# Page numbers read without a range check per page, the page table clamped once beforehand

## The reference

```
mla_past = cache_mla[li, page_table].reshape(db, PAST_LEN, MLA_KV_LORA + MLA_ROPE)
old = cache_kv[li, page_table, :, 0:2].reshape(B, PAST_LEN, 2, G, d)   # keys and values to compress
page = page_table[bi, ip // sub][..., None]                            # of the selected blocks
kp = cache_kv[li, page, rows, 2, gsel]
vp = cache_kv[li, page, rows, 3, gsel]
```

## Time and profile before

| | us |
|---|---|
| median of 3 runs | 3161.9 |
| lowest and highest run | 3148.9, 3181.5 |
| span of the profiled execution | 3163.9 |

### The profile page before, as it was taken

One profiled execution on the slowest core, in us unless ns is written; L12 is line 12 of the kernel. 1 busy time (PEld: TensorE's weight loads), 2 busy tenths in 40 slices (PEclk: granted clock), 3 DMA queues, 4 the chain that ended last, 5 costly groups with the idle time before them and its releaser, 6 DMA issues. The chain is left out here.

```text
span 3163.9 us, 69355 instructions
## 1 busy us (share of the span) xinstructions
PE 2792.1 (88%) x25382; PEld 1845.6 (58%) x25382; DVE 1249.9 (40%) x3286; ACT 875.3 (28%) x2098; POOL 124.2 (4%) x217
## 2 busy tenths in 40 slices
PE   6999888899982699799997999799999998888878
PEld 4556455666651544455466879667676765555534
DVE  3111455455546521111000000275757576666633
ACT  1111444333332010101000000164646464444400
POOL 0000000011102000000000000000000000221100
PEclk9999999999995699899987999798989898899989
DMA  4001100377753131511054766400000001777732
GB/s 174 22 12 49 29 1 1 117 222 220 227 159 48 38 133 62 211 45 41 31 157 138 231 221 190 116 2 2 2 1 2 2 2 50 224 229 219 228 123 77
DMA packets 312746, 320.72 MB, mean 101 GB/s; under 512 B 72420, under 2 KB 289940, under 8 KB 312089
## 3 DMA queue, kind: packets, MB, share of 16 engines
q1 hardware_dynamic: 226120, 233.29, 24.2%
q10 hardware_dynamic: 86290, 83.01, 8.6%
HBM read 289.15 MB, written 30.27 MB: 101 GB/s over the span
## 5 line engine op out<-in xcount | busy, mean ns | idle before, releaser
L2207 PE MATMUL bank<-cm_room 64*64 64x114 f32 (+1 forms) x4608 | 297.0, 441 | 6.6 <-DMA cm_room<-cache_nsa_kv 6.6
L2207 PEld LDWEIGHTS bank<-cm_room 64*64 64x64 f32 x4608 | 254.6, 163 | 45.9 <-DMA cm_room<-cache_nsa_kv 7.5
L2554 ACT ACTIVATE np_p<-bank,np_nmax 128x640 f32<-128x640 f32 (+7 forms) x256 | 179.3, 700 | 230.1 <-DVE np_nmax L2609 229.0
L2027 PE MATMUL bank<-cm_room 128*128 128x512 f32 (+3 forms) x576 | 224.9, 551 | 0.0
L2493 PEld LDWEIGHTS bank<-kv,np_pT 128*64 128x64 f32 x4224 | 149.3, 142 | 90.1 <-ACT np_pT L2563 42.0
L2493 PE MATMUL bank<-kv,np_pT 128*64 128x64 f32 x4224 | 185.1, 233 | 2.3 <-ACT np_pT L2563 2.2
L2609 DVE TENSOR_REDUCE np_nmax<-bank 128x1 f32<-128x640 f32 (+7 forms) x256 | 181.2, 708 | 8.8
L2479 PE MATMUL bank<-ident,np_p 128*128 128x128 f32 x1056 | 179.2, 296 | 3.7 <-ACT np_pcT L2574 3.0
L315 PE MATMUL bank<-ev_hT,ev_w 128*128 128x384 f32 (+1 forms) x576 | 173.4, 460 | 6.1 <-ACT zaT L258 6.1
L2027 PEld LDWEIGHTS bank<-cm_room 128*128 128x128 f32 (+1 forms) x576 | 103.9, 182 | 117.3 <-issue 106.4
L2563 ACT ACTIVATE np_pT<-bank 128x512 f32<-128x512 f32 (+3 forms) x384 | 160.5, 458 | 39.2 <-PE bank L2479 39.2
(11 more groups left out here) (516 smaller groups left out, 4066.2 us busy)
## 6 DMA issues: line engine op xcount, KB each, us to landing
ms_pg<-cache_mla SPq DMA_DIRECT2D x388, 144.0 KB, 2.7
ns_pg<-cache_nsa_kv SPq DMA_DIRECT2D x320, 128.0 KB, 2.8
cm_room<-cache_nsa_kv ACTq DMA_DIRECT2D x262, 128.0 KB, 4.1
cm_room<-cache_nsa_kv SPq DMA_DIRECT2D x250, 128.0 KB, 4.5
ns_pg<-cache_nsa_kv ACTq DMA_DIRECT2D x192, 128.0 KB, 3.2
ms_pg<-cache_mla ACTq DMA_DIRECT2D x124, 144.0 KB, 3.3
ev_w<-w_in_even SPq DMA_DIRECT2D x8, 768.0 KB, 10.0
cm_room<-w_in_odd SPq DMA_DIRECT2D x24, 256.0 KB, 6.9
```

The source lines that it names most:

```text
L2027: t = nc.tensor.matmul(bank[:n, f, 0:hi - lo], hT[:, i // 3 % 2, k, at:at + n], wt[:, k, lo:hi], start=k == 0, stop=k == KD - 1)
L2207: t = nc.tensor.matmul(out(blk)[kind * HD:(kind + 1) * HD], phi[blk * BLK:(blk + 1) * BLK, kind, x, :], rows(kind, blk, x), start=x == 0, ...
L2554: nc.scalar.activation(p[:, u % NPS, :width(u)], scores_ps(u)[:, :width(u)], ACT.Exp, bias=nmax[:, u % NST:u % NST + 1], accum_out=den[:, ...
```

## The change

load_constants gets one VectorE instruction that waits for the four loads, raises the numbers in c["pages"] to at least 0 and lowers them to at most 639. The four places that read page numbers pass a reason for leaving out the range checks. With it the register operation and the assert for each number are not put into the stream; the load of the numbers and the issue of the pages stay as they are.

```diff
--- before.py
+++ after.py
@@ -27,6 +27,7 @@
 PAST, PAGE = 8192, 128
 NPAGE = PAST // PAGE
 POOL = (DB * NPAGE * 5 + 3) // 4
+CLAMPED = "load_constants clamps every page number to the pool on the chip"
 EPS = 1e-6
 NEG = -1e30
 
@@ -96,6 +97,11 @@
             sp.dma_start(c["winlow"][:], a["c_winlow"]).then_inc(s_load, 16)
             sp.dma_start(c["pages"][:], a["page_table"].rearrange("b p -> (b p)").unsqueeze(0)).then_inc(s_load, 16)
             sp.wait_ge(s_load, 64)
+
+        @block.vector
+        def _(dve):
+            dve.wait_ge(s_load, 64)
+            nc.vector.tensor_scalar(c["pages"][:], c["pages"][:], 0.0, float(POOL - 1), ALU.max, ALU.min)
 
 
 class Ring:
@@ -555,7 +561,7 @@
                 for lo, key in ((0, "c_rope_sinT"), (ROPE, "c_rope_cosT"), (NOPE, "c_rope_cosT"), (QD, "c_rope_sinT")):
                     sp.dma_start(trig[lo:lo + ROPE], a[key]).then_inc(s_trig, 16)
                 for first, at in ((0, 0), (4, 4), (8, 8), (3 * NPAGE // 4, 12)):
-                    _, pages = nc.values_load_multi_w_load_instructions(c["pages"][0:1, first:first + 4], engines=[mybir.EngineType.SP], min_val=0, max_val=POOL - 1)
+                    _, pages = nc.values_load_multi_w_load_instructions(c["pages"][0:1, first:first + 4], engines=[mybir.EngineType.SP], min_val=0, max_val=POOL - 1, skip_runtime_bounds_check_because=CLAMPED)
                     for j, page in enumerate(pages, at):
                         sp.dma_start(f["pg0"][:, j, :], a["cache_mla"][0, ds(page, 1)].rearrange("a p r -> (a p) r")).then_inc(f["s_group"][at // 4], 16)
 
@@ -896,7 +902,7 @@
 
         def numbers(kind, first, count):
 
-            _, pages = nc.values_load_multi_w_load_instructions(c["pages"][0:1, first:first + count], engines=[kind], min_val=0, max_val=POOL - 1)
+            _, pages = nc.values_load_multi_w_load_instructions(c["pages"][0:1, first:first + count], engines=[kind], min_val=0, max_val=POOL - 1, skip_runtime_bounds_check_because=CLAMPED)
             return pages
 
         def s5_loads(sp):
@@ -2157,7 +2163,7 @@
     pg = phi_room(early)[1]
     for first in range(lo, hi, 16):
         last = min(first + 16, hi)
-        _, pages = nc.values_load_multi_w_load_instructions(c["pages"][0:1, n * CU + first:n * CU + last], engines=[kind], min_val=0, max_val=POOL - 1)
+        _, pages = nc.values_load_multi_w_load_instructions(c["pages"][0:1, n * CU + first:n * CU + last], engines=[kind], min_val=0, max_val=POOL - 1, skip_runtime_bounds_check_because=CLAMPED)
         for j, page in enumerate(pages, first):
             eng.dma_start(pg[:, n % 2, j, :], a["cache_nsa_kv"][0, ds(page, 1)].rearrange("a p k g d -> (a p) (k g d)")[:, 0:2 * KVW]).then_inc(early["s_page"][n % 2], 16)
 
```

## The result

| | before | after |
|---|---|---|
| median of the runs, us | 3170.9 (4 runs) | 3048.2 (4 runs) |
| lowest and highest run, us | 3148.9, 3181.5 | 3043.9, 3056.7 |
| span of the profiled execution, us | 3163.9 | 3042.0 |

The ratio is 0.963, with a 95% interval of 0.960 to 0.966. The same kernel measured a second time, against other runs of before, gave 0.9676 (0.9653 to 0.9699). The second is the better figure: two of the four runs of before in the first table (3179.9 and 3181.5) lie above all 45 that were measured later, whose medians are 3157.7 to 3159.7 us.

The account below looks back on a forecast made before the run. Page-issuing queues SP and ACT, slowed by range checks, were taken to bound the page-reading stages, not PE or DMA. Cached MLA 30 + compression 20 + cached NSA 46 - clamp 0.7 = 95 us; 3163.9 - 95 = 3069 us, range 3040 to 3112.

Parts of the forecast that it names:

- The rival of full DMA engines: DMA engines have no more to give, so waits for pages stay; 35 us gained, 3129 us; chance 0.13.
- The clamp: One VectorE instruction ahead of the first barrier, about 0.56 us, 0.6 to 1.2 with wait and branch; 0.7 us lost.
- Cached MLA, steady part: 621 to 922 us: without checks SP no longer delays PE; 22 us gained, bounds 8 and 26.
- SP falls off the path by a wide margin and PE's own work is late next: Steady cached MLA, per sample: SP needs 30.5 us without checks, PE 39.3 us, against 43.0 us.
- Its start and end: Cached MLA: start gains 5 us of PE's waits for ACT and SP's pages; end moves with PE plus 2.8 us.
- PE's gap before the S5 stage should grow: Sign at the end of cached MLA: the 17.62 us gap grows, since SP's tail stays at 50 us.
- Compression: Beginning 11 us (bounds 5 and 12) from ACT's checks behind the barrier, later 9 us (5 and 13); together 20 us.
- the 7.5 us per unit that SP loses: Later compression: SP's 29 pages lose 7.5 us of checks per unit, more than any wait there.
- Cached NSA: Samples lose 5.86 of 40.35 us, 41 us taken (bounds 22 and 55), plus 5 us at its beginning; together 46 us.
- if only the 2.87 us go, 22: Cached NSA, lower bound: only PE's 2.87 us wait per sample for ACT's checks goes, 22 us gained.
- The rival of another link: Cached NSA: ACT's order holds PE up once SP doesn't; half that stage's gain goes, 3092 us; chance 0.10.
- The sum: Whole kernel: 30 + 20 + 46 - 0.7 = 95 us gained; all bounds at once 49 and 122 us saved.

Follow-up runs that it names:

- ACT's checks in short runs: Changed kernel with ACT's checks kept, ACT reading numbers in runs of 4 and 3 rather than 16 and 12; ratio to before 0.9821.

## Why the prediction was right, and where it was not

**What bounds the kernel.** The medians of 3048.2 and 3054.0 us lie in the range of 3040 to 3112 and some 15 to 21 us below the forecast of 3069. Right: the queues that read page numbers were the limit in the three stages. With the checks gone SP waits for PE, and the DMA engines deliver up to 299 GB/s. The rival of full DMA engines (a time of 3129) has fallen.

**The clamp.** 0.41 us for the instruction and 0.4 us later at the barrier, against the 0.7 assumed.

**Cached MLA, steady part.** The size was about right: a sample went from 43.0 to 39.0 us, 27.6 us in seven, with 22 taken and bounds of 8 and 26. The bound was too low because I took PE's own 39.3 us and then cut the result for caution; PE, without idle time and at full clock, needed just that. The step "SP falls off the path by a wide margin and PE's own work is late next" was wrong as a reason. The earlier trace rows says that SP hardly waited, and I read it as if SP alone set the pace. ACT's block did so just as much: the run with SP alone free gained 0.2 us per sample there. The result only holds since the change frees both at once.

**Its start and end.** The start gained 8.2 us, not 5, because the waits for SP's pages behind the two that I named went too. The end gained the 2.8 us that I forecast: from the last group of line 1014 (1020) to the S5 stage 48.1 us passed before and 45.3 after. Yet "PE's gap before the S5 stage should grow" was wrong: it shrank from 17.62 to 7.78 us. SP's tail did stay (6 us of pages and 44 us of small loads), but PE came later. (Before, PE had ended at 952.3 us; the 953.0 of the prediction is the end of VectorE's copy behind it.) SP now issues its last pages without delay, so its small loads start, at 884.85 us, 1.2 us ahead of ACT's last four pages instead of 1.3 us behind the first of them. Thus log_dt comes ahead of the last page and holds it up; PE waits 5.28 us for it and then works at a granted clock that is low for a while (0.61 in the 5 us behind the wait, 0.87 over 887 to 924 us, 0.91 in 922 to 953 us before). I had put down nothing for a transfer that changes places with another.

**Compression.** Beginning 10.2 us (11 taken), rest 7.9 us (9 taken). The beginning is right in place: with SP alone free the wait behind ACT's block stays, at 16.69 us. For the rest I named the 7.5 us per unit that SP loses; it is as good to take the checks from ACT, with SP keeping its own (7.1 of the 7.9 us), so that reason was only half of it.

**Cached NSA.** 47.1 us against 46, for the reasons given when both queues are free: 6.0 us per sample, of which I had 5.86. The lower bound, "if only the 2.87 us go, 22", was wrong: without ACT's checks alone the stage was 2.8 us shorter, which is no more than it differs between profiles anyway, since SP paced it. The rival of another link, which wanted 38 us per sample or half the gain, has fallen: 34.5.

**The sum.** Forecast 95, profile 122. Of the 27 us between them 16 are the prompt's NSA, a term that I didn't have; 9 are the MLA, 2 the S5 stage, 1 the cached NSA, less 2 in compression. Without the 16 us the span would have been 3058, and the bounds of all terms together (122) were just met. By the second ratio the gain is 102 us rather than 122, since the profiles of the changed kernel are of its fastest runs; that is nearly what the three stages with pages gained (96 forecast, 103.8 measured). Luck has a part in it: the term of the steady MLA part held only because the change frees both queues, which the reasoning with SP alone didn't ask for. SP alone, as reasoned, gave 9.4 us in that whole stage. That the clock in a stage that the change doesn't touch would be granted otherwise was outside the sum.

## What to carry to other kernels

Where two queues feed one engine, find out for each what it allows by itself, and take the later of the two; a gain for one of them may be worth nothing until the other has it too, and then both together give more than the sum of their own (MLA 9.4 and 1.2 us alone, 38.6 together). It can also be the other way round: in the rest of compression either queue alone gave the whole 7 to 8 us. Only the run with each queue alone tells which it is. A queue that never waits is a limit, but not necessarily the only one. Look at what stands at the seam of two stages: a transfer that is harmless behind the last page costs 5 us when a faster queue puts it a microsecond ahead of it. And before a gain in a stage that the change doesn't touch is booked, see whether the profiled run is a usual one.

## What the runs showed of the hardware

- A load of page numbers into registers takes long, and not by the count alone: in the cached MLA 0.31 us for 4 numbers (ACT's checks in short runs) and 1.02 us for 16 on ACT; in the cached NSA 0.70 us for 3 and 0.79 us for 12 on ACT, but 1.64 us for 10 on SP.
- The 4 KB loads of log_dt, the same 16 numbers in pieces of 4 bytes for 64 partitions, land after 12 to 21 us, and most 144 KB pages issued in the 9 us behind one needed 7 to 19 us instead of 3; the issues of two queues were held up by 11 and 25 us, while the DMA engines as a whole were busy to 0.05 to 0.11. Loads of lambda, of the same size and pieces but with numbers of their own for each partition, landed in 3.2 to 5.9 us when issued singly among the pages and held up none.
- TensorE's granted clock in a stage with the same instructions gave 88 to 127 us at 1.2 GHz in the profiles of kernels that differ only ahead of it, 655 to 673 us of length. Two profiles of the changed kernel agreed to within 1 us there, but not in the first stretch of the program (588.5 and 584.7 us). A stage that a change doesn't touch may so move by up to 18 us, as much as a real change may bring.
